# Four convolution tiles on TensorE quadrants, a triangular corner product, the convolution's layer norm inside the chunk loop, and its output layer right behind the loop

## The chip, the cores and the metric

The kernel runs on one core of a Trainium2 chip. Its engines work beside each other: TensorE (PE in the profile, PEld its weight loads), VectorE (DVE), ScalarE (ACT), GpSimd (POOL), and SyncE (SP), whose queue issues most DMAs. They meet only at semaphores. The metric is the device time of one execution in microseconds; a lower time is better. Differences below about 0.2% can't be told from no change.

## What is computed

Two blocks of a language model over 256 tokens with 1024 features in float32. The change lies in the first block, which mixes a recurrent head layer (RWKV) with a convolution branch:

```python
def conformer_conv(p_c, dw, dw_b, ln_w, ln_b, w_o):
    u, gate = jnp.split(p_c, 2, axis=-1)
    c = u * jax.nn.sigmoid(gate)
    c = <causal depthwise convolution of c with dw, 31 taps> + dw_b
    c = jax.nn.silu(layer_norm(c, ln_w, ln_b))
    return c @ w_o

# end of rwkv7_time_mix: y (per head) from the recurrence wkv7
    y = ((y - mu) * lax.rsqrt(var + GN_EPS)) * gn_w + gn_b      # mean and variance per head
    return ((y + bonus) * g) @ w_o                             # bonus = (sum of r*k*r_k) * v

    merged = sigmoid(z_rwkv) * y_rwkv + sigmoid(z_conv) * y_conv
    x = x + rms_norm(merged @ w_out, post_mix_norm)
```

The recurrence runs over 8 chunks of 32 tokens. Inside a chunk it needs the inverse of a unit lower-triangular 32x32 matrix for each of 16 heads and 8 chunks.

## The kernel before

Activations lie transposed: a tile is 128 features by 256 tokens, and 1024 features are 8 tiles, one `slot` of the array `pj`. A large product (`pe_layer`) goes in blocks of 128 output columns. The weights of a block are split into a high part by ACT (`act_head`, L476) and a rest by DVE (`dve_rest`, L482), and PE makes 24 products of 128x256 for the block (L441 to L443; L2215 to L2217 for the layer `z`, which is spread over the chunk loop). Sums in plain float32 (`mm`) cost two records each in the trace.

The order is written out by hand, engine by engine; semaphores tie the programs together. Around the change it is this.

- Ahead of the loop DVE makes the gated input of the convolution (L1533) and signals it. PE then convolves three tiles of it (`PE_TILES = 3`): for each tap one float32 product with a 128x128 diagonal matrix as weights (L2268), 31 to a tile. ACT makes the diagonals from the identity matrix (`tap_weights`, L920) in a ring of 12 and brings the sums out (`conv_tile`, L924).
- Meanwhile DVE ends the inverses. The two 16x16 diagonal blocks are done by substitution (L1492, L1494), the corner by two triple products in 4 slabs each (`slab`, L1478 a product of 128x1024 and L1479 its sum). Both factors are triangular, and the slabs use their full squares.
- PE turns the inverses (L2279), then the chunk loop begins. DVE convolves the other five tiles: of its 31 taps, 11 ahead of the loop (`DVE_EARLY`), and the rest behind the chunk work of the first six iterations, `DVE_TAPS = (4, 4, 3, 3, 3, 3)`. A tap is one instruction a tile (L1550). `scale_keys(1)` (L1568) stands ahead of the last three early taps; PE's `chunk_keys(1)` waits for it.
- One iteration on PE: x from the last state (L2293, L2297), `chunk_keys` (L2126), two blocks of `z`, y from the old state (L2308), u (L2320), `chunk_products` of the next chunk (L2239), the state's update (L2331), y from this chunk (L2335). DVE copies half of u (L1600), masks the products (L1559) and adds to the state (`state_sum`, L1575), which the next x waits for.
- The layer norm of the convolution: its mean is summed on PE in iteration 6 (L2121) and subtracted on DVE in iteration 7 (L1597); ACT squares it there.
- Behind the loop, in this order on PE: the sum for the variance (L2121), the mean per head (`head_sums`, L2115), the bonus (L2346), the variance per head of squares made by POOL (L707), and only then the layer `conv_out`. Beside these DVE scales, centres and multiplies, ACT makes a sigmoid and a linear form of each tile (L973, L974), then the roots of the head norm (L986). The rest of the head norm (POOL L709, ACT L995, DVE L1652 and L1654) lies beside `conv_out`, and `rwkv_out` takes its result.

## Time and profile before

| | us |
|---|---|
| median of 3 runs | 1449.87 (1447.17 to 1450.07) |
| the profiled execution, device time | 1448.39 |
| its span in the trace | 1446.7 |
| PE busy | 1363.5 (94%) |
| DVE busy | 1036.3 (72%) |
| ACT busy | 766.1 (53%) |
| POOL busy | 110.3 (8%) |

The span runs from the first to the last instruction in the trace; 1.7 us of the device time lie around it. The times of all rows are microseconds from the start of the span. A matmul's own time in the trace holds some 0.2 us of latency and overlaps the next, so PE's pace is read from starts.

### The profile page before, as it was taken

The page shows a single profiled execution, that of the slowest core. Times are in us where ns is not written, and L with a number is a line of the kernel's source. Part 1 is how long each engine was busy: PE and PEld are TensorE (multiplying, and loading weights), DVE is VectorE, ACT ScalarE, POOL GpSimd, SP SyncE. Part 2 cuts the span into 40 slices and gives each one's busy share as a digit, 9 for nine tenths or more (in the row PEclk, how much of TensorE's full clock was granted, in tenths as well). Part 3 has the DMA queues.
Part 4 walks back from the last instruction along what each step waited for, and adds up shares of the span by engine and source line. Part 5 has one row for each costly group of instructions (what it writes and reads, how often), then busy time and mean ns, then how long its engine had stood idle before and what let it go on. Part 6 is the DMA issues. An engine that isn't in the chain of part 4 may idle for free.

```text
span 1446.7 us, 29631 instructions
## 1 busy us (share of the span) xinstructions
PE 1363.5 (94%) x12191; PEld 1303.9 (90%) x12191; DVE 1036.3 (72%) x1707; ACT 766.1 (53%) x1262; POOL 110.3 (8%) x127
## 2 busy tenths in 40 slices
PE   6998999898799999999998899999999989999998
PEld 6997988897698999998998699999999978999986
DVE  5769798995677666458598977787565655787754
ACT  5584384334655544345467655544454545644543
POOL 2000000000200211000010100211000100011100
PEclk9999999998899999999999899999999999999999
DMA  8634510120154563854484245554765621455462
GB/s 263 185 97 137 174 61 2 61 90 31 59 175 146 177 192 98 263 182 149 140 249 131 88 147 175 175 174 128 227 193 154 208 84 59 148 191 185 161 212 79
DMA packets 199151, 211.55 MB, mean 146 GB/s; under 512 B 8634, under 2 KB 190666, under 8 KB 198874
## 3 DMA queue, kind: packets, MB, share of 16 engines
q1 hardware_dynamic: 196938, 201.39, 43.8%
q0 software_dynamic: 2000, 8.46, 2.0%
q8 instruction: 88, 1.44, 0.4%
q14 instruction: 29, 0.24, 0.0%
q10 hardware_dynamic: 96, 0.02, 0.0%
HBM read 208.22 MB, written 1.64 MB: 145 GB/s over the span
## 4 chain that ended last, share of the span: by engine, by line
PE 76%; DVE 12%; issue 5%; ACT 3%; DMA 2%; POOL 1%; SPq 0%; DVEq 0%; ACTq 0%; POOLq 0%
PE pb L441 19%; PE pb L443 18%; PE pb L442 18%; PE pb L2268 3%; DVE w_lo L482 2%; DVE pj L1550 1%; PE pb L2586 1%; PE pb L2588 1%; PE pb L2587 1%; PE pb L2126 1%; DMA raw<-in_ffn_w_down_dram 1%; PE pb L2513 1%; PE pb L2169 1%; PE pb L2115 1%; PE pb L2121 1%
## 5 line engine op out<-in xcount | busy, mean ns | idle before, releaser
L441 PE MATMUL pb<-x_hi,w_hi 128*128 128x256 f32 x1984 | 567.1, 286 | 16.7 <-DVE w_lo L482 6.3
L482 DVE TENSOR_TENSOR w_lo<-raw,w_hi 128x1024 fp32r<-128x1024 f32 (+2 forms) x384 | 469.0, 1224 | 157.7 <-ACT w_hi L476 156.9
L476 ACT ACTIVATE w_hi<-raw 128x1024 fp32r<-128x1024 f32 (+2 forms) x384 | 395.7, 1040 | 333.7 <-PE pb L443 251.1
L442 PE MATMUL pb<-x_lo,w_hi 128*128 128x256 f32 x1984 | 563.6, 284 | 0.0
L443 PE MATMUL pb<-x_hi,w_lo 128*128 128x256 f32 x1984 | 563.5, 284 | 0.0
L441 PEld LDWEIGHTS pb<-x_hi,w_hi 128*128 128x128 f32 x1984 | 383.2, 193 | 20.8 <-DVE w_lo L482 11.7
L442 PEld LDWEIGHTS pb<-x_lo,w_hi 128*128 128x128 f32 x1984 | 383.4, 193 | 0.2
L443 PEld LDWEIGHTS pb<-x_hi,w_lo 128*128 128x128 f32 x1984 | 383.1, 193 | 0.0
L716 POOL TENSOR_TENSOR sub<-sub,rstd 128x256 f32<-128x256 f32 x66 | 72.0, 1106 | 575.1 <-ACT sub L1045 575.1
L441 PE MATMUL pb<-act_hi,w_hi 128*128 128x256 f32 x392 | 111.9, 285 | 3.8 <-DVE w_lo L482 3.8
L443 PE MATMUL pb<-act_hi,w_lo 128*128 128x256 f32 x392 | 111.6, 285 | 0.0
L442 PE MATMUL pb<-act_lo,w_hi 128*128 128x256 f32 x352 | 100.3, 285 | 0.0
L1045 ACT ACTIVATE sub<-sub 128x256 f32<-128x256 f32 x66 | 26.5, 415 | 101.1 <-DVE sub L1759 84.4
L441 PEld LDWEIGHTS pb<-act_hi,w_hi 128*128 128x128 f32 x392 | 76.0, 194 | 4.3 <-DVE w_lo L482 4.3
L443 PEld LDWEIGHTS pb<-act_hi,w_lo 128*128 128x128 f32 x392 | 75.9, 194 | 0.0
L442 PEld LDWEIGHTS pb<-act_lo,w_hi 128*128 128x128 f32 x352 | 68.3, 194 | 0.0
L1730 DVE TENSOR_TENSOR sub<-pb,rstd 128x256 f32<-128x256 f32 x66 | 27.8, 423 | 45.8 <-PE pb L443 43.4
L1550 DVE SCALAR_TENSOR_TENSOR pj<-pj,par 128x255 f32<-128x255 f32 (+29 forms) x150 | 59.6, 464 | 0.8
L1736 DVE TENSOR_TENSOR sub<-pb,sub 128x256 f32<-128x256 f32 x66 | 27.7, 420 | 39.7 <-PE pb L443 22.2
L1336 DVE TENSOR_TENSOR pj<-pb,rstd 128x256 f32<-128x256 f32 x72 | 30.3, 422 | 31.5 <-PE pb L443 30.1
L1052 ACT ACTIVATE act_hi<-sub 128x256 f32 (+1 forms) x66 | 27.3, 416 | 45.1 <-DVE sub L1736 44.8
L2126 PE MATMUL pb<-ident,pj 128*128 128x128 f32 (+1 forms) x218 | 37.1, 313 | 8.2 <-DMA pj<-in_x_dram 6.0
(340 smaller groups left out, 2186.1 us busy)
## 6 DMA issues: line engine op xcount, KB each, us to landing
raw<-in_ffn_w_up_dram SPq DMA_DIRECT2D x55, 1024.0 KB, 5.1
raw<-in_w_in_dram SPq DMA_DIRECT2D x28, 1024.0 KB, 5.1
raw<-in_ssd_w_in_dram SPq DMA_DIRECT2D x20, 1024.0 KB, 5.4
raw<-in_ffn_w_down_dram SPq DMA_DIRECT2D x16, 1024.0 KB, 5.3
raw<-in_fox_w_in_dram SPq DMA_DIRECT2D x16, 1024.0 KB, 5.7
raw<-in_ffn_w_down_dram SPq DMA_DIRECT2D x16, 896.0 KB, 5.3
raw<-in_ffn_w_gate_dram SPq DMA_DIRECT2D x11, 1024.0 KB, 5.3
raw<-in_ssd_w_out_dram SPq DMA_DIRECT2D x8, 1024.0 KB, 5.5
```

Source lines behind the costliest of these rows:

```text
L441: pe.matmul(o, w_hi[m][:, k, :], hi[:, k0 + k, :], start=first and k == 0, stop=False)
L442: pe.matmul(o, w_hi[m][:, k, :], lo[:, k0 + k, :], start=False, stop=False)
L443: mm = pe.matmul(o, w_lo[m][:, k, :], hi[:, k0 + k, :], start=False, stop=final and k == nk - 1)
L476: act.activation(piece(ly, w_hi[m], nk, m), raw_piece(ly, s, nk, m), ACT.Copy).then_inc(sem("w_hi_ready"), 1)
L482: dve.tensor_tensor(piece(ly, w_lo[m], nk, m), raw_piece(ly, s, nk, m), piece(ly, w_hi[m], nk, m).bitcast(F32), ALU.subtract).then_inc(sem ...
L716: pool.tensor_tensor(s_tile[m], s_tile[m], rstd[:, :], ALU.mult).then_inc(sem("glu_silu"), 1)
L1336: tt(o, pb[m][:, 0:T], rstd[:, :], ALU.mult).then_inc(sem("evac_done"), 1)
L1550: go(stt(o[:, s:T], c[:, 0:T - s], w, o[:, s:T], ALU.mult, ALU.add))
L1730: tt(g_tile[m], pb[m][:, 0:T], rstd[:, :], ALU.mult).then_inc(sem("evac_done"), 1)
L1736: tt(a_tile[m - 2], pb[m][:, 0:T], s_tile[m - 2], ALU.mult).then_inc(sem("evac_done"), 1)
L2126: return pe.transpose(o, i, ident[0:n, 0:n])
L2268: mm(pb[4 + k % 2][:, s:T], diag[(CONV_TAPS * k + s) % NDIAG], slot(U)[:, k, 0:T - s], start=s == 0, stop=s == CONV_TAPS - 1, skip_group_c ...
```

## The change

Six parts.

1. `PE_PAIRS = 2`: PE convolves four tiles, in two pairs. For `ug`, the layer that makes u and gate, the weight pieces of units 0 and 2 are taken in another order of columns (`raw_piece`), so that of a pair's 256 features the tile c holds those with a = 0, 1 at partitions 64a, of which the convolution's outputs are partitions 64c of bank a. A tap of a pair is four products of 64x64 weights, one to each quadrant of the array. The weights are 64 columns wide (`ident2`, `conv_dw_pe`), two tiles of them to a tap, in a ring of 24.
2. DVE convolves four tiles, 15 taps ahead of the loop, 16 in iterations 0 to 3.
3. The corner: the slabs leave out what the triangles make zero; shapes go from 4x16x16 down to a quarter. The evacuations of the first two `z` blocks move ahead of it.
4. The layer norm: mean in iteration 4, variance and root in iteration 5, scaling in iteration 6, all sums in bank 5, and a Silu of ACT instead of sigmoid, linear form and product.
5. Behind the loop PE makes the bonus and the head mean, then begins `conv_out`; the head variance is summed behind its second block. The squares go from POOL to ACT, the root's product from POOL to DVE. The rows of `z_rwkv` get their sigmoid in iteration 4.
6. Five DMAs more on SP in the load of the parameters (four of `conv_dw_pe`, one for a split row), ahead of the third weight unit.

PE, where the convolution begins. Before, from the products of chunk 0 on:

```order
L2239 MATMUL pb<-pj 64x64 x16
L2126 MATMUL pb<-ident,pj 128x128 x8
L2268 MATMUL pb<-pj 128x256
L2268 MATMUL pb<-pj 128x255
L2268 MATMUL pb<-pj 128x254
```

Now:

```order
L2292 MATMUL pb<-pj 64x64 x16
L2179 MATMUL pb<-ident,pj 128x128 x8
L2324 MATMUL pb<-pj 64x256 x4
L2324 MATMUL pb<-pj 64x255 x4
L2324 MATMUL pb<-pj 64x254 x4
```

A tap is four products of 64 columns for two tiles, where it was one product of 128 for one; 62 such groups stand where 93 products stood.

DVE, the early taps and `scale_keys(1)` ahead of the loop. Before:

```order
L1550 SCALAR_TENSOR_TENSOR pj<-pj,par 128x249 x5
L1568 TENSOR_TENSOR pj<-pj,chunk_decay 128x512
L1550 SCALAR_TENSOR_TENSOR pj<-pj,par 128x248 x5
L1550 SCALAR_TENSOR_TENSOR pj<-pj,par 128x247 x5
L1550 SCALAR_TENSOR_TENSOR pj<-pj,par 128x246 x5
L1526 TENSOR_TENSOR pj<-pb,rstd 128x256 x2
```

Now:

```order
L1599 SCALAR_TENSOR_TENSOR pj<-pj,par 128x245 x4
L1617 TENSOR_TENSOR pj<-pj,chunk_decay 128x512
L1599 SCALAR_TENSOR_TENSOR pj<-pj,par 128x244 x4
L1599 SCALAR_TENSOR_TENSOR pj<-pj,par 128x243 x4
L1599 SCALAR_TENSOR_TENSOR pj<-pj,par 128x242 x4
L1575 TENSOR_TENSOR pj<-pb,rstd 128x256 x2
```

The scaling of the keys of chunk 1 stood behind 8 taps of 5 instructions, and stands behind 12 taps of 4.

PE, the end of the loop and what follows. Before:

```order
L2320 MATMUL pb<-pj 32x64 x16
L2335 MATMUL pb<-pj 64x32 x16
L2121 MATMUL pb<-pj,ones 128x256 x8
L2115 MATMUL pb<-pj,blk 128x256 x8
L2346 MATMUL pb<-small,ident 64x256 x16
L2115 MATMUL pb<-sub,blk 128x256 x8
L441 MATMUL pb<-x_hi,w_hi 128x256
```

Now:

```order
L2375 MATMUL pb<-pj 32x64 x16
L2396 MATMUL pb<-pj 64x32 x16
L2402 MATMUL pb<-small,ident 64x256 x16
L2168 MATMUL pb<-pj,blk 128x256 x8
L445 MATMUL pb<-x_hi,w_hi 128x256
```

Two of the four sums between the loop and `conv_out` are gone from there: one is in the loop, one behind two blocks of the layer.

```diff
-        PE_TILES, NDIAG, DIAG_LEAD = 3, 12, 8
-        diag = [slot(ZC)[:, i // 2, P * (i % 2):P * (i % 2) + P] for i in range(NDIAG)]
+        PE_TILES, NDIAG, DIAG_LEAD = 2 * PE_PAIRS, 24, 8
+        diag = [slot(ZC)[:, i // 4, HEAD * (i % 4):HEAD * (i % 4) + HEAD] for i in range(NDIAG)]
-        DVE_TAPS = (4, 4, 3, 3, 3, 3)
+        DVE_TAPS = (4, 4, 4, 4)
+        LN_SUM, LN_VAR, LN_SCALE = len(DVE_TAPS), len(DVE_TAPS) + 1, len(DVE_TAPS) + 2
...
+            if ly.name == "ug" and u % PE_PAIRS == 0:
+                pair = raw[s][:, 0:nk, 2 * P * (m // 2):2 * P * (m // 2) + 2 * P]
+                return pair.rearrange("p k (a c i) -> p k a c i", c=2, i=HEAD)[:, :, :, m % 2, :]
... POOL
-            pool.tensor_tensor(tmp2, slot(R), slot(R), ALU.mult).then_inc(sem("pool_stages"), 1)
-            pool.tensor_tensor(slot(R), slot(R), slot(TMP), ALU.mult).then_inc(sem("pool_stages"), 1)
... ACT: the diagonals
-                    act.activation(diag[n % NDIAG], ident[:, :], ACT.Copy, scale=par_col("conv_dw", KC * (CONV_TAPS - 1 - s) + k)).then_inc(sem("tap_ready"), 1)
+                    for c in range(2):
+                        n = 2 * (CONV_TAPS * q + s) + c
+                        if n >= NDIAG and c == 0:
+                            act.wait_ge(sem("tap_summed"), (n - NDIAG) // 2 + 1)
+                        act.activation(diag[n % NDIAG], ident2[:, :], ACT.Copy,
+                                       scale=par_col("conv_dw_pe", 2 * (CONV_TAPS * q + CONV_TAPS - 1 - s) + c)).then_inc(sem("tap_ready"), 1)
... ACT: inside the loop
+                if c == LN_SUM:
+                    act.wait_ge(sem("evac_done"), L["z"].evac0 + BANKS + KC)
+                    act.activation(slot(ZR), slot(ZR), ACT.Sigmoid).then_inc(sem("z_ready"), 1)
+                if c == LN_VAR:
+                    log_exp()
+                    act.wait_ge(sem("ln_centred"), 2)
+                    act.activation(slot(U), slot(GATE), ACT.Square).then_inc(sem("ln_act"), 1)
+                if c == LN_SCALE:
+                    for m in range(2):
+                        act_head(act, L["conv_out"], 0, 0, m)
+                    for k in range(KC):
+                        if k % 4 == 0:
+                            act.wait_ge(sem("ln_ready"), k // 4 + 1)
+                        act.activation(slot(GATE)[:, k, :], slot(GATE)[:, k, :], ACT.Silu, scale=par_col("conv_ln_w", k),
+                                       bias=par_col("conv_ln_b", k)).then_inc(sem("ln_act"), 1)
                 act.wait_ge(sem("u_done"), c + 1)
... ACT: beside conv_out
+            def gn_stages(u, m):
+                if (u, m) == (0, 0):
+                    <4 squares of 128x512, as the head mean is subtracted>
+                if (u, m) == (0, 1):
+                    <8 products of g with gn_w>
+                if (u, m) == (0, 2):
+                    <wait for the variance; 4 pairs of Ln and Exp of 128x512>
+                if (u, m) in ((0, 3), (1, 0)):
+                    <4 tiles each of y_hi>
... DVE: the corner
-                rows = left[:, r, :].unsqueeze(2).broadcast_to([P, SLAB, BLOCK, BLOCK])
+            def corner_columns(i):
+                n, r = SLAB * (i + 1), slice(SLAB * i, SLAB * i + SLAB)
+                products(lt_corner[:, :, r], lt_corner[:, :, 0:n], mt[:, BLOCK:BLOCK + n, BLOCK + SLAB * i:BLOCK + n], (BLOCK, SLAB, n))
+            def corner_rows(i):
+                r, j = slice(SLAB * i, SLAB * i + SLAB), slice(SLAB * i, BLOCK)
+                products(mt_corner[:, r, :], mt[:, r, j], lt_corner[:, j, :], (SLAB, BLOCK, BLOCK - SLAB * i))
... DVE: inside the loop
+                if c == LN_SCALE:
+                    dve.wait_ge(sem("ln_act"), 2)
+                    for h in range(2):
+                        tt(cv[:, 4 * h:4 * h + 4, :], cv[:, 4 * h:4 * h + 4, :], rs[:, :].unsqueeze(1).broadcast_to([P, 4, T]),
+                           ALU.mult).then_inc(sem("ln_ready"), 1)
...
+                if c == LN_SUM:
+                    dve.wait_ge(sem("ln_mean"), 1)
+                    ts(rs[:, :], pb[5][:, 0:T], 1.0 / D, None, ALU.mult).then_inc(sem("ln_centred"), 1)
+                    dve.wait_ge(sem("ln_centred"), 1)
+                    tt(cv, cv, rs[:, :].unsqueeze(1).broadcast_to([P, KC, T]), ALU.subtract).then_inc(sem("ln_centred"), 1)
... PE
-                    mm(pb[4 + k % 2][:, s:T], diag[(CONV_TAPS * k + s) % NDIAG], slot(U)[:, k, 0:T - s],
+                    for c in range(2):
+                        for a in range(2):
+                            ins = mm(pb[4 + 2 * q + a][side[c], s:T], diag[(2 * i + c) % NDIAG][side[a], :],
+                                     slot(U)[side[a], 2 * q + c, 0:T - s], start=s == 0, stop=s == CONV_TAPS - 1, skip_group_check=True)
...
+                if c == LN_SUM + 1:
+                    pe.wait_ge(sem("ln_centred"), 1)
+                if c == LN_VAR + 1:
+                    pe.wait_ge(sem("ln_act"), 2)
...
+                if c == LN_SUM:
+                    pe.wait_ge(sem("conv_ready"), PE_TILES + 1)
+                    feature_sums(pb[5][:, 0:T], slot(GATE)).then_inc(sem("ln_mean"), 1)
+                if c == LN_VAR:
+                    pe.wait_ge(sem("ln_act"), 1)
+                    feature_sums(pb[5][:, 0:T], slot(U)).then_inc(sem("ln_var"), 1)
...
+            def group_sums(u, m):
+                if (u, m) == (0, 1):
+                    pe.wait_ge(sem("gn_act"), 4)
+                    head_sums(tmp2, 4).then_inc(sem("gn_var"), 1)
```

In angle brackets stands in words what the lines do.

## Rows read from the trace of the kernel before

**Rows 1.** The page: busy tenths of 40 slices, with PE's granted clock.

```profile
PE   6998999898799999999998899999999989999998
PEclk9999999998899999999999899999999999999999
```

**Rows 2.** Stretches: start:end, length, busy of PE, PEld, DVE, ACT, POOL; clock, DMA.

```profile
188.90:237.30 48.40, 47.06 (x455) 43.39 (x459) 47.18 (x65) 34.93 (x91) 0.53 (x1) 0.96 0.08 25
...
296.20:308.80 12.60, 12.49 (x283) 11.91 (x286) 12.04 (x25) 5.95 (x12) 0.00 (x0) 1.00 0.19 58
...
340.10:349.40 9.30, 4.86 (x161) 4.36 (x161) 7.22 (x7) 6.14 (x10) 0.00 (x0) 0.67 0.20 57
349.40:377.60 28.20, 18.99 (x80) 14.29 (x80) 16.59 (x32) 22.26 (x37) 3.71 (x1) 0.74 0.06 20
```

**Rows 3.** PE in order of time: start, length, line, tiles, shape, count [idle before].

```profile
188.92 39.77 PE L2268 MATMUL pb<-pj 128*128 128x256 f32 x186 [3.21 <-DVEq L1534]
...
237.22 0.69 PE L2293 MATMUL pb<-pj 32*32 32x64 f32 x32 [0.74 <-issue]
238.22 1.06 PE L2126 MATMUL pb<-ident,pj 128*64 128x128 f32 x8
...
282.26 1.91 PE L2126 MATMUL pb<-ident,pj 128*64 128x128 f32 x8
```

**Rows 4.** PE in order of time, products on parts of the array.

```profile
340.88 0.46 PE L2297 MATMUL pb<-sub,pj 64*32 64x64 f32 x32
...
358.45 3.67 PE L2346 MATMUL pb<-small,ident 16*64 16x256 f32 x32
```

**Rows 5.** ACT in order of time.

```profile
11.54 3.29 ACT L776 ACTIVATE x_hi<-x_res,par 128x256 fp32r<-128x256 f32 x8
...
182.71 3.60 ACT L920 ACTIVATE pj<-ident,par 128x128 f32<-128x128 f32 x12
```

**Rows 6.** DVE in order of time: the corner, early taps, state sums.

```profile
184.87 0.95 DVE L1492 TENSOR_TENSOR sub<-sub 128x450 f32<-128x450 f32 x1
185.86 0.62 DVE L1494 TENSOR_REDUCE sub<-sub 128x30 f32<-128x450 f32 x1
...
192.26 1.98 DVE L1478 TENSOR_TENSOR sub<-sub 128x1024 f32<-128x1024 f32 x1
194.27 1.22 DVE L1479 TENSOR_REDUCE sub<-sub 128x64 f32<-128x1024 f32 x1
195.52 1.99 DVE L1478 TENSOR_TENSOR sub<-sub 128x1024 f32<-128x1024 f32 x1
...
236.59 0.69 DVE L1568 TENSOR_TENSOR pj<-pj,chunk_decay 128x512 f32<-128x512 f32 x1
237.20 6.13 DVE L1550 SCALAR_TENSOR_TENSOR pj<-pj,par 128x248 f32<-128x248 f32 x15
...
249.90 0.69 DVE L1575 TENSOR_TENSOR sub<-sub,pb 128x512 f32<-128x512 f32 x1 [0.21 <-DVE pj L1559]
...
295.32 0.69 DVE L1575 TENSOR_TENSOR sub<-sub,pb 128x512 f32<-128x512 f32 x1 [0.22 <-PE pb L2331]
```

**Rows 7.** PE in order of time, behind the loop.

```profile
347.44 1.92 PE L2335 MATMUL pb<-pj 64*64 64x32 f32 x32 [4.33 <-issue]
349.29 5.78 PE L2121 MATMUL pb<-pj,ones 128*128 128x256 f32 x16
354.91 3.62 PE L2115 MATMUL pb<-pj,blk 128*128 128x256 f32 x16
...
377.60 0.58 PE L441 MATMUL pb<-x_hi,w_hi 128*128 128x256 f32 x1 [5.98 <-ACT pj L986]
```

**Rows 8.** PE in order of time, the last block of `conv_out` and `rwkv_out`.

```profile
401.70 0.58 PE L441 MATMUL pb<-x_hi,w_hi 128*128 128x256 f32 x1 [2.30 <-DVE w_lo L482]
...
405.63 0.28 PE L441 MATMUL pb<-x_hi,w_hi 128*128 128x256 f32 x1
405.98 0.28 PE L441 MATMUL pb<-y_hi,w_hi 128*128 128x256 f32 x1
```

More of the change, by code:

```diff
@@ L678, in _ @@
             sync()
+            for h in range(2):
+                rows = slice(HEAD * h, HEAD * h + HEAD)
+                link(pool.tensor_copy(ident2[rows, :], ident[rows, rows]))
             for b in range(4):
@@ L941, in _, with conv_heads @@
                                pb[4 + i][:, :].rearrange("p (t y) -> p y t", y=32), ACT.Copy).then_inc(sem("inverse_rows"), 1)
+            def conv_heads(first, last):
+                act.wait_ge(sem("block_done"), L["z"].item1 + BANKS)
+                for k in range(first, last):
+                    act.wait_ge(sem("ln_act"), 2 + k + 1)
+                    act.activation(x_hi[:, k, :], slot(GATE)[:, k, :], ACT.Copy).then_inc(sem("x_hi_ready"), 1)
             v_rows(0)
@@ L992, in y_heads @@
+            log_exp()
+            def gn_stages(u, m):
+                if (u, m) == (0, 0):
+                    for b in range(4):
+                        act.wait_ge(sem("gn_dve"), 4 + b + 1)
+                        act.activation(tmp2[:, 2 * b:2 * b + 2, :].rearrange("p k t -> p (k t)"), pair(R, b), ACT.Square).then_inc(sem("gn_act"), 1)
                 if (u, m) == (0, 1):
-                    act.wait_ge(sem("pool_stages"), GN_ROOTED)
                     for k in range(KC):
-                        act.activation(slot(R)[:, k, :], slot(R)[:, k, :], ACT.Identity, scale=par_col("gn_w", k),
-                                       bias=par_col("gn_b", k)).then_inc(sem("gn_root"), 1)
@@ L997, in y_heads @@
-                if (u, m) == (0, 3):
-                    act.wait_ge(sem("mix_in"), KC + 1)
-                    for k in range(KC):
-                        act.activation(y_hi[:, k, :], slot(R)[:, k, :], ACT.Copy).then_inc(sem("x_hi_ready"), 1)
-            act_layer(act, L["conv_out"], y_heads, nxt=L["rwkv_out"])
+                        act.activation(slot(U)[:, k, :], slot(G)[:, k, :], ACT.Copy, scale=par_col("gn_w", k)).then_inc(sem("gn_act"), 1)
+                if (u, m) == (0, 2):
+                    act.wait_ge(sem("gn_var"), 1)
+                    for b in range(4):
+                        link(act.activation(pair(TMP, b), pb[4 + b][:, :], ACT.Ln, bias=eps[:, 2:3], scale=1.0 / HEAD))
+                        act.activation(pair(TMP, b), pair(TMP, b), ACT.Exp, scale=-0.5).then_inc(sem("gn_root"), 1)
@@ L1003, in mixed_head @@
+                if (u, m) in ((0, 3), (1, 0)):
+                    for b in range(2 * u, 2 * u + 2):
+                        act.wait_ge(sem("mix_in"), b + 1)
+                        for k in (2 * b, 2 * b + 1):
+                            act.activation(y_hi[:, k, :], slot(R)[:, k, :], ACT.Copy).then_inc(sem("x_hi_ready"), 1)
+            act_layer(act, L["conv_out"], gn_stages, nxt=L["rwkv_out"])
             def mixed_head(j):
-                act.wait_ge(sem("mix_in"), KC + 1 + j + 1)
+                act.wait_ge(sem("mix_in"), 4 + j + 1)
```

219 lines of the change are left out of this document (103 added, 116 removed).

## The prediction

> **What bounds the kernel now.** I read the page's slices first: PE is busy nearly everywhere, with its clock granted in full (2.4 GHz, digit 9), but for the tenth and eleventh slice, 326 to 398 us, where the clock digit is 8 and PE's own are 8 and 7 (once more near 800 us, in another part) [rows 1]. So the kernel is PE-bound outside, and only what shortens PE's own path there, or fills its gaps, counts. The table by stretches shows where the path is thin [rows 2]. From 188.9 to 237.3 PE and DVE are both full: PE convolves (39.77 us for 93 taps) [rows 3] and then turns the inverses, DVE works 47.2 of 48.4 us. In the loop a good iteration takes 12.6 us, PE and DVE both over 12. The last one and the stretch behind the loop (28.2 us) are not full on any engine: a chain of small steps handed from engine to engine, with a mean clock of 0.67 and 0.74, so for half of the time or more at the lower level, 1.2 GHz. Everything from `rwkv_out` on (406.0 us) [rows 8] is untouched by the diff, so the gain is the lead with which that layer starts. I follow this lead past six marks.
>
> **1. The corner on DVE.** A slab costs 3.26 us from product to next product (192.26 to 195.52) [rows 6]; there are eight, 26.1 us. Now their sizes are 1024, 768, 512, 256, twice. The pair of 450 elements (0.95 and 0.62) and the pair of 1024 (1.98 and 1.22) [rows 6] give lines through which I read 2.55, 1.8 and 1.1 us for the smaller ones, gaps included. Sum 2 x 8.75 = 17.5 us, so DVE is 8.6 us earlier. Ahead of `scale_keys(1)` stand 48 tap instructions now, not 40, at 6.13 / 15 = 0.41 us each [rows 6]: 3.3 us back. It ended at 237.3 and ends at 232.1, a lead of 5.2. The moved evacuations (two instructions) cost DVE the same either way.
>
> **2. The taps on PE.** The taps take 0.40 to 0.43 us each for a full-width product of some 240 columns (39.77 / 93) [rows 3]. A tap of a pair is four products of 64x64, and the question is how many run at once. The nearest row is L2297: 16 products of 64 columns on tiles of 64x32, eight places of the array, 0.46 us from the first start to the last end [rows 4]. One full-width product of 64 columns would be 0.107 us at the taps' pace, sixteen 1.7 us. So rows and columns of the array both work in parallel, far more than fourfold. L2346, 256 columns long but on two places only, takes 3.67 / 16 = 0.23 us a product, half of 0.43 [rows 4], so long products share too. I take full concurrency: 62 taps at 0.405, plus the 2.3 us that the low clock costs at the start (39.77 less 93 x 0.403), 27.4 us. PE is through at 216.5, not 228.7. Bounds: two at a time, 0.81 us (the L2346 case), and one at a time, 1.62. The Trainium skill, page "TensorE: Matmul & The Clock Gate", section "Measured speedup vs the span model", has 3.07 times for four tiles in four row groups, not 4. By that a tap would be 0.53 us, the taps 7.5 us longer, and the sum the same within 1 us, because of the slack in the next paragraph; no row here has four places.
>
> **ACT must feed it.** A scaled copy costs 0.41 us at 256 columns and 0.30 at 128 (3.29 / 8, 3.60 / 12) [rows 5]; I extrapolate 0.24 to 0.25 for 64. Per tap of a pair 0.48, slower than PE's 0.405, but 12 taps lie ready when PE starts (24 of them, 5.7 us, fit between 182.7 and 188.9), and with two weight pieces first, ACT falls behind only at the very end: about 216.5 too. If the narrow copy gained nothing (0.30), ACT ends at 221.5.
>
> **3. Where the loop starts.** From the end of the taps to x of chunk 0 it was 8.5 us (228.7 to 237.2) [rows 3], so x now begins at 225.1, keys(1) a microsecond later, and there PE **waits for DVE's `scale_keys(1)` until 232.1**: the 12 us that the quadrants win are cut to a lead of 6.1 (keys(1) started at 238.2) [rows 3]. This is the slack that hides a slower tap, up to 0.5 us a tap. The idle 6 us cost clock: after such a gap the same eight turns took 1.91 us, not 1.06 [rows 3], and the first products behind them ran slow too; 1.7 us. `state_sum(0)` came 11.7 us behind the start of the keys (249.9) [rows 3, 6], now at 245.5: lead 4.4.
>
> **4. Iterations 0 to 3** are set by DVE. Between state sums 0 and 3 lay 45.4 us (249.90 to 295.32) [rows 6] with 20, 20 and 15 tap instructions; now 16 each, 7 fewer, 2.9 us: 42.5. I take 14.0 us each, 42.0, since in the third PE, not DVE, came last ("<-PE L2331") and had a gap to close. Lead 7.8.
>
> **5. Iterations 4 to 7.** They took 54.0 us (295.3 to 349.4) [rows 6, 7] with one sum of 8 tiles in it, 3.6 us at full clock, as the like sum L2115 took [rows 7], and the 4.3 us idle of PE ahead of its last products [rows 7]. Now a second sum comes in (+3.6); PE waits for the mean to leave bank 5, behind `state_sum(4)` (+1.1), and for ACT in iteration 6, which makes eight Silus ahead of its copies of u (+0.8). The first two waits hold back x and all behind it on PE; ACT's Square, table load and root fit beside two blocks of `z`. Gone are the 4.3 us idle and about 2.5 us of low clock (clock 0.67 in the last iteration) [rows 2]. DVE has no taps there any more. Sum -1.3: 52.7 us, lead 9.1, loop end 340.3.
>
> **6. Behind the loop** 28.2 us [rows 2, 7] become the bonus, 3.67 [rows 4], and the head mean, 3.62 [rows 7]: 7.3 us. The tiles of x_hi and x_lo (8 x 0.3 on ACT, 8 x 0.34 on DVE) fit beside. Low clock may come back, as L2121 took 5.78 at the same place where the like sum took 3.62 [rows 7]; I put 1 us. Gain 28.2 - 8.3 = 19.9, lead 29.0, `conv_out` starts near 348.5. It took 28.4 us (377.60 to 405.98) with a wait of 2.30 for weights and a slow start [rows 7, 8]; now 8 blocks at 24 x 0.12 = 2.88 us (405.63 to 405.98 is three products) [rows 8] and the variance sum, 3.6: 26.7. Lead **30.7**.
>
> What else is there costs nothing as I see it. In `conv_out` DVE has some 8 x 0.34, 12 x 0.6 and 8 x 0.34 us of head norm between eight weight rests and eight gates, about 27 in 26.7 + the next layer's slack; the nearest deadline, the rests of block (1,2), is met by 2 us. SP issues five small DMAs more at about 0.35 us, 1.8 us, with PE's turn of the parameters near behind; between 0 and 2 us, I take 0, since the weights that follow are wanted much later. The other order of columns in `raw_piece` changes no size.
>
> **The sum.** 1446.7 - 30.7 = 1416.0 of span, with 1.7 around it 1417.7 against the profiled 1448.39. The median is 1.5 above that run, so the forecast is **1419**.
>
> **Rivals.** (a) *Two quadrants at a time*: 0.81 us a tap. For it speaks that no row has four places at this length; against it L2297. PE is through at 241.4, keys(1) begin 9.5 later without a gap, `state_sum(0)` at 262.6: 17 later than forecast, 1436. (b) *Quadrants one after another*, since each product adds to a bank that another one writes: 1.62 us a tap, 62 taps 100 us, `state_sum(0)` near 312, **slower, 1486**. It decides from 1.03 us a tap on, where 62 taps end at 255.0 and `state_sum(0)` comes at 276.2, 30.7 behind forecast. L2297 writes banks the same way and speaks against it. (c) *ACT feeds too slowly*: at 0.40 us a copy, as a paced one might take, 50 pairs are 40 us, PE is through at 232, +8: 1427. (d) *The head norm beside `conv_out` is late*, DVE's queue holding a weight rest behind a wait for ACT's roots: 2 to 6 us, 1423. (e) *The loop is better than I think*: PE follows DVE without the low clock, -4 us: 1415. (f) That the change doesn't shorten the chain at all: no, two of the four sums and POOL's two steps are gone from it.
>
> **Chances.** Forecast with (d) and (e), which are its margins: 0.80; (c) 0.06; (a) 0.09; (b) 0.03; something unseen of 5 to 25 us 0.02. The range takes the forecast's margins and (c), and the lower half of (a): 1411 to 1434. Faster by over 0.2% (about what a measurement of this kernel can tell) 0.95, same 0.01, slower 0.04.
>
> **What would show it.** Taps: 62 groups from 188.9 that end near 216.5; if they end near 241, (a). An idle of PE of about 6 us ahead of keys(1), ended by DVE's scaling; without it step 3 is wrong. Corner 17.5 us. State sums near 245.5 and 287.5. Bonus right behind the loop, `conv_out` near 348.5 and `rwkv_out` near 375, without a POOL row between. I would be wrong most of all by PE's clock, which I only take from like places, and by the waits in iterations 4 to 6.

## The result

The changed kernel takes **1424.66 us** (median, 1423.21 to 1429.6), the kernel before 1448.62 us in the same series: ratio 0.9857, 95% interval 0.9831 to 0.9883. It is faster, as forecast, and 5.7 us above the 1419 that were named, inside the range. The profiled run has a span of 1424.0 us, and 8.0 us more than the 1416.0 of the sum have to be found in it.

The page's slices of the changed kernel, the ones of [rows 1] again:

```profile
PE   5999997999999999999998899999999998999998
PEclk8999998998999999999999899999999999999999
```

The weak place of two slices is now one, the tenth (320 to 356 us, clock digit 8). But the first slice went from 6 to 5 with clock digit 8, and the seventh (214 to 249 us), which was at 9 with full clock, is at 7 with clock digit 8: that is PE's wait ahead of the loop. In order of time (start, length in us, engine, line, tiles, count, idle before and who ended it), first SP's queue and PE at the start of the kernel, then PE from the taps to the loop, then one state sum of DVE and the second product of u in iteration 7, with all that stands between it and `conv_out`:

```profile
13.40 6.67 SPq L597 DMA_DIRECT2D pj<-in_conv_dw_dram  x6
25.28 0.52 SPq L597 DMA_DIRECT2D pj<-in_ffn_conv_b_dram  x1
27.11 1.51 PE L2179 MATMUL pb<-ident,pj 128*128 128x128 f32 x6 [3.51 <-DMA pj<-in_ffn_conv_b_dram]
...
192.71 27.26 PE L2324 MATMUL pb<-pj 64*64 64x256 f32 x496 [2.12 <-DVEq L1583]
219.90 6.03 PE L2335 MATMUL pb<-ident,sub 128*32 128x32 f32 x256
236.05 1.92 PE L2179 MATMUL pb<-ident,pj 128*64 128x128 f32 x8 [7.16 <-DVE pj L1617]
250.45 0.69 DVE L1624 TENSOR_TENSOR sub<-sub,pb 128x512 f32<-128x512 f32 x1 [0.21 <-DVE pj L1608]
...
347.06 1.24 PE L2396 MATMUL pb<-pj 64*64 64x32 f32 x32 [0.96 <-DVE pj L1650]
348.23 7.09 PE L2402 MATMUL pb<-small,ident 16*64 16x256 f32 x32
355.25 5.14 PE L2168 MATMUL pb<-pj,blk 128*128 128x256 f32 x16
360.03 0.47 PE L445 MATMUL pb<-x_hi,w_hi 128*128 128x256 f32 x1
```

Read against [rows 3, 6 to 8], the leads over the kernel before are, in us:

| mark | forecast | changed kernel | run e11 (below) |
|---|---|---|---|
| weight blocks on PE and DVE behind the start (36 us) | 0 | -5.0 | -2.0 |
| the taps on PE begin | 0 | -3.8 | -2.0 |
| `state_sum(0)` | 4.4 | -0.5 | 4.0 |
| `state_sum(3)` | 7.8 | 2.5 | 7.7 |
| end of the loop | 9.1 | 1.1 | 10.6 |
| `conv_out` starts | 29.0 | 17.6 | 28.6 |
| `rwkv_out` starts | 30.7 | 19.3 | 30.3 |
| end of the span | 30.7 | 22.7 | 29.2 |

So four things came late: the start (3.8 us where the taps begin), the clock between the keys of chunk 1 and `state_sum(0)` (1.0 more than forecast), the iterations 4 to 7 (2.8), and the stretch behind the loop (3.4). The rest of the table is as forecast. The start itself was 5.0 us late; some 1.2 of it was gone before the taps, most of it at one place. The data of the inverses go out to DRAM and back, and DVE waits for them. The same two transfers took 11.9 us before and 10.9 now; what made them shorter stays open. First a weight rest of DVE behind the start and the second transfer before, then the same now:

```profile
31.34 1.23 DVE L482 TENSOR_TENSOR w_lo<-raw,w_hi 128x1024 fp32r<-128x1024 f32 x1
...
154.79 7.38 DMA sub<-sub_in
```

```profile
36.38 1.23 DVE L491 TENSOR_TENSOR w_lo<-raw,w_hi 128x1024 fp32r<-128x1024 f32 x1 [0.67 <-ACT w_hi L485]
...
159.53 6.49 DMA sub<-sub_in
```

Behind `rwkv_out`, where both kernels run the same instructions, the lead grew by 3.4 us. That part isn't the change's: over the profiled runs of this study the same part gave between -1.1 and +6.1 us, with the clock of a few stretches (0.93 from 720 to 800 us here, 0.91 in the same work before). It is also why medians of kernels that differ by 2 or 3 us overlap. Below, the marks in the traces decide, and the times are given beside them. The marks scatter too: in seven profiled runs whose instructions are the same up to the taps, these begin between 192.7 and 193.5 us, and in two others with one start (e11, e12) 1.5 us apart. Of the times alone, only e7's interval lies clear of the changed kernel's.

### The profile page after: what moved, and what is told of

The parts are those of the page before. It is cut to its first block, busy times and chain, and to the rows that moved or that the text cites. A ratio compares the mean times of both kernels' runs of the same rounds, so it can differ in the third digit from the quotient of the medians.

```text
span 1424.0 us, 30260 instructions
## 1 busy us (share of the span) xinstructions
PE 1348.2 (95%) x12502; PEld 1280.9 (90%) x12502; DVE 1013.9 (71%) x1680; ACT 762.1 (54%) x1294; POOL 102.4 (7%) x127
## 4 chain that ended last, share of the span: by engine, by line
PE 78%; DVE 13%; issue 4%; ACT 2%; DMA 2%; SPq 2%; DVEq 0%; ACTq 0%; POOLq 0%
PE pb L445 20%; PE pb L447 19%; PE pb L446 19%; DVE pj L1599 2%; DVE w_lo L491 2%; PE pb L2646 1%; PE pb L2645 1%; PE pb L2644 1%; PE pb L2179 1%; PE pb L2168 1%; SPq L597 1%; DMA raw<-in_ffn_w_down_dram 1%; PE pb L2571 1%; PE pb L2268 1%; PE pb L2269 1%
## 5 line engine op out<-in xcount | busy, mean ns | idle before, releaser
L485 ACT ACTIVATE w_hi<-raw 128x1024 fp32r<-128x1024 f32 (+2 forms) x384 | 396.2, 1040 | 336.9 <-PE pb L447 256.8
L1783 DVE TENSOR_TENSOR sub<-pb,rstd 128x256 f32<-128x256 f32 x66 | 27.7, 423 | 46.6 <-PE pb L447 43.9
L1789 DVE TENSOR_TENSOR sub<-pb,sub 128x256 f32<-128x256 f32 x66 | 27.7, 419 | 39.8 <-PE pb L447 22.2
L1091 ACT ACTIVATE act_hi<-sub 128x256 f32 (+1 forms) x66 | 27.3, 416 | 44.7 <-DVE sub L1789 44.7
L2179 PEld LDWEIGHTS pb<-ident,pj 128*128 128x128 f32 (+1 forms) x219 | 28.3, 153 | 24.2 <-issue 8.9
```

The costliest lines, as they stand in the source:

```text
L485: act.activation(piece(ly, u, w_hi[m], nk, m), raw_piece(ly, u, s, nk, m), ACT.Copy).then_inc(sem("w_hi_ready"), 1)
L1091: act.activation(o, a_tile[m], ACT.Copy).then_inc(sem("act_hi_ready"), 1)
L1783: tt(g_tile[m], pb[m][:, 0:T], rstd[:, :], ALU.mult).then_inc(sem("evac_done"), 1)
L1789: tt(a_tile[m - 2], pb[m][:, 0:T], s_tile[m - 2], ALU.mult).then_inc(sem("evac_done"), 1)
L2179: return pe.transpose(o, i, ident[0:n, 0:n])
```

## The experiments

Each is the changed kernel with one edit, unless it says otherwise. The state sums (us from the span's start) of all the runs, the end of the loop, and the start of `conv_out`:

| | sum 0 | 1 | 2 | 3 | 4 | 5 | 6 | loop ends | `conv_out` | median us | ratio to before, interval |
|---|---|---|---|---|---|---|---|---|---|---|---|
| changed | 250.5 | 264.4 | 279.0 | 292.8 | 308.6 | 328.6 | 342.1 | 348.3 | 360.0 | 1424.66 | 0.9857, 0.9831 to 0.9883 |
| e1 | 249.6 | 263.6 | 277.5 | 291.3 | 307.0 | 324.1 | 337.6 | 345.9 | 359.2 | 1423.49 | 0.9855, 0.981 to 0.9899 |
| e2 | 248.3 | 265.1 | 279.6 | 293.4 | 309.1 | 326.2 | 339.7 | 347.6 | 359.7 | 1426.01 | 0.9859, 0.9819 to 0.9898 |
| e3 | 250.0 | 264.4 | 278.3 | 293.9 | 310.0 | 326.2 | 339.7 | 346.0 | 357.9 | 1420.84 | 0.9826, 0.9787 to 0.9865 |
| e4 | 250.6 | 265.2 | 279.1 | 293.3 | 309.4 | 326.5 | 340.0 | 354.3 | 360.5 | 1425.91 | 0.9854, 0.9812 to 0.9896 |
| e5 | 248.0 | 262.4 | 276.3 | 291.9 | 308.1 | 326.7 | 340.2 | 348.3 | 360.1 | 1425.36 | 0.9849, 0.9815 to 0.9883 |
| e6 | 248.6 | 263.1 | 277.0 | 292.6 | 308.7 | 327.3 | 340.8 | 348.9 | 360.7 | 1426.91 | 0.9858, 0.9823 to 0.9893 |
| e7 | 258.3 | 272.7 | 286.6 | 302.2 | 318.3 | 336.9 | 350.4 | 358.6 | 370.3 | 1435.4 | 0.993, 0.9904 to 0.9956 |
| e8 | 248.4 | 262.3 | 276.2 | 290.0 | 305.8 | 322.9 | 336.4 | 342.1 | 354.0 | 1421.28 | 0.9842, 0.9807 to 0.9877 |
| e9 | 248.5 | 262.4 | 276.3 | 290.1 | 305.9 | 324.5 | 338.0 | 343.7 | 355.5 | 1423.14 | 0.9832, 0.9813 to 0.9852 |
| e10 | 245.5 | 259.4 | 273.3 | 287.1 | 302.9 | 321.5 | 335.0 | 344.0 | 355.9 | 1422.82 | 0.9831, 0.98 to 0.9862 |
| e11 | 245.9 | 259.9 | 273.7 | 287.6 | 303.3 | 319.4 | 333.0 | 338.8 | 349.0 | 1419.5 | 0.9811, 0.9788 to 0.9835 |
| e12 | 244.5 | 259.1 | 273.4 | 287.3 | 303.0 | 319.1 | 332.7 | 341.9 | 353.9 | 1420.57 | 0.9812, 0.9789 to 0.9835 |

### The start: e1, e5, e6

e1 issues the four loads of `conv_dw_pe` on ACT's queue, e5 leaves them on SP's but last of the list, e6 puts them on POOL's:

```diff
 e1, e6: load_params(sp, range(1, par_tiles), "par_loaded", pairs=False)
 e1: @block.scalar, behind par_first
+    load_params(act, range(1, par_tiles), "par_loaded", pairs=True)
 e5: behind the list without them
+    load_params(sp, range(1, par_tiles), "par_loaded", pairs=True)
 e6: @block.gpsimd, behind the constants
+    load_params(pool, range(1, par_tiles), "pairs_loaded", pairs=True)
```

> The four loads of the pair-ordered convolution weights (62 rows of two-way split 256-byte pieces, 15.5 KB each) are issued on ACT's queue at the start of the kernel and no longer on SP's queue ahead of weight unit 2; nothing else changes. Theory A (SP's issue of these four is what makes the start 5.0 us later): SP's last parameter load is issued near 19 to 20 us instead of 25.3, PE's turn of the parameters comes without its idle of 3.5 us, everything behind is 4 to 5 us earlier, the time 1420 us (4.5 less than the changed kernel's 1424.7). Rival B (the extra cost is the transfers' own, small pieces that hold up whatever shares the DMA engines): the loads then delay x or the first weight unit instead, and the time stays at 1424 to 1427.

> The four loads of the pair-ordered convolution weights stay on SP's queue but come last of the parameter loads, behind ffn_conv_b, at about 19 us. Theory A (an issue of such a load is long only while the DMA engines are full with weights, to 19 us here; on SP in the changed kernel four took about 5.8 us, on ACT's queue in the run before 9.7 us): there, with the DMA engines nearly idle, each takes 0.4 to 0.5 us, the last parameter lands at 23 to 24 us instead of 27.1, and all behind is 3 us earlier: 1421.5. Rival B (the issue is long for its 62 pieces of 256 bytes themselves, 1.4 us or more each wherever it stands): the last parameter lands at 26 to 27 us and the time is the same, 1424.

> The four loads of the pair-ordered convolution weights are issued on POOL's queue, behind its constants (7.7 us), where POOL waits for squares until 17.7 us; SP's list is then that of the kernel before, but one more piece each of conv_b, conv_w. Theory A (the 5.0 us at the start come from the issue of these four alone): the last parameter lands near 21 to 22 us, PE's turn of the parameters is not waited for, everything behind is 4 to 5 us earlier, 1420. Rival B (POOL's own issue takes as long as on the other queues, 9 us and more, and its sum of squares comes later): 1424 or later.

e1 in order of time, the four loads on ACT's queue:

```profile
3.23 9.72 ACTq L599 DMA_DIRECT2D pj<-in_conv_dw_dram  x4
```

e5, the same on SP's queue, and PE's turn of the parameters:

```profile
19.40 2.72 SPq L599 DMA_DIRECT2D pj<-in_conv_dw_dram  x4
...
24.92 1.51 PE L2182 MATMUL pb<-ident,pj 128*128 128x128 f32 x6 [1.37 <-DMA pj<-in_conv_dw_dram]
```

e6, the loads on POOL's queue, and the turn:

```profile
8.51 5.29 POOL L599 DMA_DIRECT2D pj<-in_conv_dw_dram  x4 [0.87 <-POOL g_mask L703]
...
25.53 1.48 PE L2182 MATMUL pb<-ident,pj 128*128 128x128 f32 x6 [2.03 <-DMA pj<-in_ffn_conv_b_dram]
```

The kernel before, its last parameter load and its turn:

```profile
19.11 0.32 SPq L582 DMA_DIRECT2D pj<-in_ffn_conv_b_dram  x1
...
23.75 0.70 PE L2126 MATMUL pb<-ident,pj 128*128 128x128 f32 x5
```

The prediction priced an issue at 0.35 us. Four loads of 62 pieces of 256 bytes took 5.9 us on SP in the changed kernel (6.67 less 0.78 for the two plain ones), 9.7 on ACT at the very start, and 2.7 at 19.4 us, when the DMA engines moved 27 GB/s. So the same issue costs 0.7 us with nearly idle DMA engines, 1.5 on average on SP and 2.4 on ACT while weights are being fetched (307 to 389 GB/s in those stretches of e1). Short pieces aren't the only cause of a long issue: the plain load of `gn_b`, right behind four weight loads, took 2.95 us in both kernels. The Trainium skill ("Perfetto Trace Analysis", section "DMA Instruction — HWDGE (DVE, Sync)") has the profiled time of a DMA instruction include the wait for the descriptor generator and the making of all its descriptors, and the DMA engines' own work not. No row here separates these parts; what the rows show is that the issue of one and the same load depends on what the DMA engines are doing.

e1 undid nothing: ACT held its own first work back for as long (DVE's first rest of the weights, right behind ACT's first high part, came 4.1 us later), and the first weight rest behind the turn stands at 29.49 us, where it was at 29.46. But e5 and e6, in which SP's list ended at 22.1 and 20.4 us instead of 25.8, were only 1.7 and 1.1 us earlier at the last rest ahead of the taps, not 3 or 5. Theory A was right on the issue and wrong on the whole. The turn of the parameters still takes 1.5 us, as in the changed kernel, not the 0.70 of the kernel before: PE has been idle, the granted clock is 0.50, there are six tiles to turn and not five, and the weight products behind it start 0.21 us apart, not 0.12. e10 (below) separates the two: filled with products nobody reads, PE turned the parameters in 0.87 us at 26.9, and the work was 1.7 us earlier right behind and 2.2 at the taps, with the landing only 0.2 earlier. e11, filled and loaded as e5, was 3.1 us earlier right behind, but only 1.8 at the taps, since there the transfers of the inverses' data took 12.5 us, and 10.9 in the changed kernel; e12, with the same start, was 3.3 earlier. **So some 2 of the 5.0 us are clock; the rest is the landing, of which reordering the loads brought 1 to 2 at the marks.** None of it shows in the times: e5 and e6 lie 0.7 and 2.3 us above the changed kernel by the medians.

### PE's wait ahead of the loop: e2, e7, e8, e9

e2 scales the keys behind 7 early taps; e7 computes the corner in full; e8 takes 18 taps of PE twice (the convolution it computes is then another one); e9 puts 14 products nobody reads in PE's wait.

```diff
 e2
-conv_taps(0, DVE_EARLY - 3); scale_keys(1); conv_taps(DVE_EARLY - 3, DVE_EARLY)
+conv_taps(0, DVE_EARLY - 8); scale_keys(1); conv_taps(DVE_EARLY - 8, DVE_EARLY)
 e7
 <both corner products with shape (SLAB, BLOCK, BLOCK), for all slabs>
 e8
-for c in range(2):
+for c in (0, 1, 0, 1) if q == 0 and 2 <= s < 20 else (0, 1):
 e9, in iteration 0 ahead of chunk_keys(1)
+for _ in range(14):
+    mm(pb[6][:, 0:T], ones[:, :], slot(U)[:, 0, :], start=True, stop=True)
```

> The corner's eight slabs are computed in full again (1024 products each, their halves of zeros included, as in the kernel before), all else as in the changed kernel. Theory A (DVE alone sets when the loop gets under way, through scale_keys(1) and the taps behind it): scale_keys(1) ends at 244.7 instead of 236.1, PE's idle ahead of keys(1) grows to 15.8 us, state_sum(0) comes 8.6 us later, 259.2, and the time is 1433. Rival B (other waits of the loop give part of it back): less than 5 us later, 1429 or below.

e7 confirms who sets the start of the loop. PE's wait for the scaling in e7, in order of time (13.89 us, it was 7.16):

```profile
244.68 1.92 PE L2179 MATMUL pb<-ident,pj 128*64 128x128 f32 x8 [13.89 <-DVE pj L1617]
```

The scaling comes 8.6 us later, `state_sum(0)` 7.8 and `conv_out` 10.3, and the median is 10.7 higher. What DVE does ahead of the loop counts in full.

> DVE scales the keys of chunk 1 behind 7 early taps instead of 12; the number of taps ahead of the loop stays 15. Theory A (PE's idle of 7.2 us ahead of keys(1) delays z, y1 and u of iteration 0, and DVE then waits for them): PE's wait shrinks to under 1 us, z of iteration 0 begins near 229 instead of 237.7, DVE comes out of its taps at 241 as now and finds z and u ready; state_sum(0) at 246.5 to 247.5 instead of 250.6, and the time is 3 to 4 us less, 1421. Rival B (DVE sets the start of the loop whatever the order, because the 15 taps are there in either case): state_sum(0) moves by under 1 us and the time stays within 1 us of 1424.7.

e2: the wait went where theory A said, `state_sum(0)` came only 2.2 us earlier, and iteration 1 took 16.9 us instead of 13.9. Nothing is left at `state_sum(1)`. PE of e2 in order of time:

```profile
241.69 1.92 PE L2369 MATMUL pb<-pj,sub 64*64 64x32 f32 x32 [5.85 <-DVE pj L1575]
```

Two stretches of e2 (start:end, length, busy of PE, PEld, DVE, ACT, POOL, granted clock, DMA):

```profile
240.00:245.00 5.00, 3.31 (x72) 3.08 (x74) 2.20 (x7) 0.27 (x1) 0.00 (x0) 0.50 0.00 0
...
250.00:255.00 5.00, 5.00 (x81) 4.40 (x77) 4.89 (x13) 1.82 (x5) 0.00 (x0) 0.50 0.02 3
```

The wait wasn't gone but moved: PE has its `z` done by 235.8 and now waits 5.85 us for DVE's taps to end. The clock is at the lower level (0.50, so 1.2 GHz) to about 255 us, and the work behind it pays. Neither theory had that. The time didn't fall (1426.01).

> 18 of the 62 taps on PE (those of number 2 to 19 of the first pair of tiles) are multiplied and added twice, so the convolution's result of tiles 0 and 1 is not the reference's; PE has 7.3 us more work in the convolution. Theory A (PE's lead there is spent waiting for DVE's scale_keys(1) in any case): PE ends its taps at 227.3 instead of 220.0, its idle of 7.2 us ahead of keys(1) is gone, state_sum(0) comes where it came (250.6) or up to 2 us earlier since the clock no longer falls in the idle time, the time is 1422.5 to 1424.7. Rival B (PE's end of the taps does matter): 7 us later, 1432.

> Ahead of keys(1) PE issues 14 products of 256 columns whose result nobody reads (lower half of bank 6, 0.43 us each, 6.0 us in all), where it now sits idle for 7.2 us. Theory A (the run with 18 taps taken twice was faster because the idle of PE there costs clock: keys 1.91 us instead of 1.06, z of iteration 0 in 7.7 us instead of 5.75): the time falls as it did there, state_sum(0) comes near 248.4 instead of 250.6, the time is 1421, and the granted clock of 235 to 245 us is 1.0. Rival B (there it was the later end of the taps, or a better draw of the low-clock stretches in the loop, that helped): state_sum(0) comes as before, the time stays at 1424.

e8, in which PE does **more** (34.58 us of taps, not 27.26), is the test of both. Its keys, in order of time:

```profile
236.66 1.06 PE L2179 MATMUL pb<-ident,pj 128*64 128x128 f32 x8
```

Those of e9:

```profile
236.76 1.06 PE L2184 MATMUL pb<-ident,pj 128*64 128x128 f32 x8 [0.42 <-DVE pj L1617]
```

And a stretch of e8, whose granted clock was 0.50 in the changed kernel:

```profile
235.00:240.00 5.00, 4.41 (x93) 4.18 (x94) 4.90 (x13) 2.81 (x7) 0.00 (x0) 1.00 0.01 3
```

7.3 us of added work cost nothing, and `state_sum(0)` came 2.1 us earlier (2.0 in e9, with the whole result right). The slack of step 3 is real. What the idle time in it costs is read from the start of these keys to `state_sum(0)`: 11.7 us in e8, e9, e10, e11 and e12, where PE doesn't idle ahead of them, as in the kernel before; 13.0 to 14.1 in e1 and e3 to e7, with the idle time, and 14.4 in the changed kernel. So it costs 1.3 to 2.7 us of clock, and the changed kernel's draw was the worst. At the marks a gain stays a gain: e8 and e9 have 13.8 to 14.0 us in each of iterations 1 to 3. In the times it isn't shown: 1421.28 and 1423.14, with intervals that overlap the changed kernel's; e9 was forecast at 1421.

### The layer norm's mean: e3

```diff
     mask_products(c + 1)
+    if c == LN_SUM: <wait for ln_mean, rs = pb[5] / D>
     state_sum(c)
```

> In iteration 4 DVE reads the layer norm's mean out of bank 5 ahead of state_sum(4) (where it sits idle for 2.1 us) instead of behind scale_keys(6). Theory A (PE's idle of 0.9 us ahead of x(5) is what drops the clock, so that x, keys and z of iteration 5 take 1.10, 1.91 and 7.4 us instead of 0.69, 1.06 and 5.75): x(5) starts 0.9 us earlier and at full clock, state_sum(5) comes 17 us behind state_sum(4) instead of 20.1, the time is 3 us less, 1421.5. Rival B (the clock falls in iteration 5 for what PE did before, the many small products, not for this idle): only the 0.9 us is gained, 1423.8.

The changed kernel in order of time, what PE waits for ahead of x of iteration 5:

```profile
310.33 1.10 PE L2354 MATMUL pb<-pj 32*32 32x64 f32 x32 [0.91 <-DVE rs L1664]
```

A stretch of the changed kernel behind it, with its clock:

```profile
314.00:319.00 5.00, 5.00 (x32) 5.00 (x32) 0.71 (x2) 4.19 (x4) 0.00 (x0) 0.68 0.00 0
```

The same product in e3:

```profile
310.84 0.69 PE L2355 MATMUL pb<-pj 32*32 32x64 f32 x32
```

Read from all the runs, the step from state sum 4 to 5 takes 16.1 us in the three runs with this edit (e3, e11, e12), 17.1 us in four without it (e1, e2, e4, e8), and 18.6 or 20.1 in the six others. So the wait costs 1.0 us by itself, which is what step 5 had for it, and in six of ten profiled runs the clock falls behind it as well, for 1.5 to 3.0 us more. Theory A has it, but as a risk, not a rule. The clock falls in other places as well: the step from state sum 2 to 3 takes 15.6 us in e3, e5, e6 and e7 and 13.8 in eight runs, with a granted clock of 0.50 for some microseconds (280 to 284 us in e3). e3 lost 1.8 us there.

### The clock behind the loop: e4, e10, e11, e12

```diff
 e4, in iteration 7
+    <4 bonus products ahead of u, 12 behind u>
 e10: as e9, and
+    <7 products of 128 columns ahead of the first sum of squares, 7 behind it>
+    <2 products of 256 columns ahead of the wait for the rows of u, iterations 6 and 7>
 e11: as e10, with the edits of e5 and e3
 e12: as e11, and the bonus
-    <16 products with 64 columns of the array (ident[0:16, h:h + 1] broadcast to 64)>
+    <8 products with 128, their pattern written by POOL in iteration 6>
```

> The 16 bonus products are issued within iteration 7, 4 of them ahead of the products of u and 12 behind, instead of behind the loop. Theory A (the lower clock behind the loop comes from PE's idle moments in iteration 7 while it waits for the copies of x and u, and filling them keeps the clock): the bonus takes about 3.7 us of which 1 lies in gaps, the head mean 3.6 instead of 5.14, conv_out starts 5 us earlier, 1419.5. Rival B (the clock is down in that stretch whatever is issued there, or the products in the loop delay y2 by as much as they save): the bonus takes 7 us, only the 1 us of gaps is gained, 1423 to 1425.

> As e9, and in three more places where PE waits: 7 products of 128 columns ahead of the first sum of squares (PE idle 2.3 us) and 7 behind it, ahead of the turn of the parameters (idle 3.5 us), and 2 of 256 columns ahead of the wait for the rows of u in iterations 6 and 7 (idle 0.9 us each). Theory A (the 5.0 us lost at the start are 3.4 us of later landing and the rest low clock: turn of the parameters 1.51 us instead of 0.70, the weight blocks at 0.21 us a product to about 31 us; the bonus's 7.09 us and the head mean's 5.14 are the low clock of the idle moments in iterations 6 and 7): 1.5 to 2 us less at the start than e9 and 3 to 5 us less behind the loop, 1415 to 1417. Rival B (the filling only keeps the clock for a moment, or comes in the way of the products that wait): 1420 to 1422, as e9.

> As e10, with the four pair-ordered loads last of the parameter loads on SP (as e5) and the layer norm's mean read ahead of state_sum(4) (as e3). Theory A (with PE filled, the clock at the start doesn't fall, and the earlier landing is worth its full 2.5 us; the wait ahead of x(5) costs 0.9 us or, in a run in which the clock falls there, 3): 2.5 to 3.5 us less than e10, 1412 to 1414. Rival B (what is gained early is given back by low-clock stretches of iterations 3 to 5, as in e5, whose lead of 2.8 us at state_sum(0) was 2.3 at state_sum(5) and nothing behind the loop): within 1 us of e10.

> As e11, and the bonus is made by 8 products with all 128 columns of the array (a 16x128 pattern that POOL writes into a free tile in iteration 6) instead of 16 with 64. In e11 PE is busy without a gap from 330 to 350 us, and the clock still falls at about 341, two microseconds into the bonus's products; the bonus takes 5.0 us and the head mean 5.7. Theory A (the clock falls there because of the products' small tiles, 16 rows by 64 columns, with nothing large beside them): with twice the columns per product the fall is later or gone, bonus 3.5 us and head mean 3.6 to 4.5, conv_out starts 2 to 3.5 us earlier than in e11 (348.96), the time is 1416.5 to 1418. Rival B (the small products of iteration 7 ahead of them decide, or the 16 rows do): bonus 5 us or more, head mean 5 to 6, the time within 1 us of e11.

PE in e4, in order of time:

```profile
344.18 1.97 PE L2344 MATMUL pb<-small,ident 16*64 16x256 f32 x8
...
347.10 5.38 PE L2344 MATMUL pb<-small,ident 16*64 16x256 f32 x24
...
352.42 1.92 PE L2408 MATMUL pb<-pj 64*64 64x32 f32 x32
```

PE in e11:

```profile
338.75 5.02 PE L2418 MATMUL pb<-small,ident 16*64 16x256 f32 x32
343.70 5.70 PE L2172 MATMUL pb<-pj,blk 128*128 128x256 f32 x16
```

Three stretches of e11:

```profile
338.00:340.00 2.00, 2.00 (x40) 1.57 (x39) 1.85 (x7) 1.14 (x4) 0.00 (x0) 1.00 1.09 381
340.00:342.00 2.00, 2.00 (x18) 1.20 (x16) 1.54 (x4) 1.98 (x3) 0.00 (x0) 0.73 0.22 62
342.00:344.00 2.00, 2.00 (x11) 0.87 (x8) 0.55 (x2) 1.99 (x2) 0.00 (x0) 0.50 0.00 0
```

PE in e12:

```profile
335.26 1.81 PE L2387 MATMUL pb<-pj,sub 64*64 64x32 f32 x29 [0.52 <-issue]
...
341.88 7.19 PE L2423 MATMUL pb<-small,pj 16*128 16x256 f32 x16
```

In e4 the bonus takes 7.3 us inside the loop, about what it took behind it, and `conv_out` starts where it did: rival B. In e10 the start and the keys keep their clock, and it falls in iteration 7, ahead of the bonus; of the 3 to 5 us that its theory A had behind the loop none came (11.9 us from the loop's end to `conv_out`, 11.7 in the changed kernel). In e11 PE is busy without a gap from 330 us to the end of the bonus, and the clock still falls, at 341 us. So idle moments alone aren't what brings it down there. e12 was to try the 64 columns of the bonus, but can't decide on them: its clock fell at 335 us, at a gap of 0.5 us, ahead of the bonus. It shows only that at the low clock 8 products of 128 columns take as long as 16 of 64 (7.19 us, and 7.09 in the changed kernel). In all the runs the last blocks of `z` are in iteration 6, and small products, sums and at most two products nobody reads follow on PE until `conv_out`. Whether that is the cause wasn't tried; it would need `z` blocks moved behind iteration 6. The fall comes between 335 and 351 us from run to run, and the stretch from the loop's end to `conv_out` takes 10.2 us (e11) to 13.3 us (e1) in the runs with the bonus behind the loop, where 8.3 was forecast; what starts it stays open.

e11 and e12 have the lowest ratios, 0.9811 and 0.9812 of the kernel before (0.9788 to 0.9835 for e11); e11 is some 5 us under the changed kernel by the median, 6.5 by the span, its interval just overlapping. It reaches the marks of the forecast within 1.5 us, `rwkv_out` at 375.7 where 375.3 was forecast, but not its own forecast of 1412 to 1414. Behind `rwkv_out` the three runs with a filled start (e10 to e12) took 1040.8 to 1041.8 us, as the kernel before did (1040.7), and the changed kernel and its nine other runs 1034.6 to 1038.8. Whether the filling does that wasn't tried. It is at least a warning that a lead at a mark isn't yet a gain in time: e10 leads e9 by 3.0 us at `state_sum(0)`, and their medians are 0.3 us apart.

## Why the prediction was right, and where not

**Corner, right.** The first four slabs take 3.29, 2.55, 1.83 and 1.09 us, 8.76 where 8.75 was forecast (the fourth stands behind two weight rests). e7 shows that they are worth what DVE gets. The first slab, the fourth and the scaling of the keys, which ends at 236.0 where 232.1 was forecast, late by the start's 3.8:

```profile
193.43 2.01 DVE L1516 TENSOR_TENSOR sub<-sub 128x1024 f32<-128x1024 f32 x1
...
203.38 0.60 DVE L1516 TENSOR_TENSOR sub<-sub 128x256 f32<-128x256 f32 x1
...
235.30 0.69 DVE L1617 TENSOR_TENSOR pj<-pj,chunk_decay 128x512 f32<-128x512 f32 x1
```

**Taps, right on the quadrants; the total is right by luck.** 27.26 us for 62 taps, forecast 27.4, and the four quadrants run as one: rivals (a) and (b) are out. But the forecast was 25.1 us of products and 2.3 of low clock at the start, and the clock was 1.00 throughout the taps. What took the 2 us was ACT. PE goes at 0.39 to 0.44 us a tap to about 208 us, then at 0.48 to the end, which is ACT's pace (46 copies in 11.09 us). 16 taps in the middle, 13 late ones, and ACT beside these:

```profile
199.67 6.52 PE L2324 MATMUL pb<-pj 64*64 64x240 f32 x128
...
209.80 6.36 PE L2324 MATMUL pb<-pj 64*64 64x246 f32 x104
```

```profile
208.22 11.09 ACT L934 ACTIVATE pj<-ident,par 128x64 f32<-128x64 f32 x46
```

PE's weight loads waited for ACT's copies 23 times, 6.3 us in all. So rival (c) holds in small: the copies cost 0.24 us as forecast, and PE waits for them in the last third of the taps and more, not "only at the very end". In the runs whose clock was low as the taps began (e3 to e6 and e9 to e11) they took 27.5 to 27.7 us, hardly longer, because ACT sets the end; and it cost nothing, because of the wait below. The prediction's reading of L2297 as "far more than fourfold" is too strong for its own figures (1.7 us against 0.46 is 3.7). The Trainium skill's 3.07 ("TensorE: Matmul & The Clock Gate", section "Measured speedup vs the span model") is for four row groups. It does not carry over to this pattern of two row groups by two column groups: before ACT holds PE back, four products take 0.39 to 0.44 us, and one full-width product took 0.40 to 0.43.

**The wait ahead of the loop, right but for 1 us of clock.** 7.16 us, forecast about 6, and the clock loss behind it 2.7 us (1.3 to 2.7 over the runs), forecast 1.7. (The row that priced it, the keys at 282.26 us in [rows 3], stood behind waits of 1.59 and 0.68 us, not behind one of 6.) `state_sum(0)` is 4.9 us late by the start's 3.8 and this 1.0. The sentence that a tap slower by 0.1 us costs nothing was right too (e8). **Iterations 0 to 3, right:** 42.4 us for 42.0. Rival (e), a loop 4 us better, is out for this run.

**The start, wrong: the term of SP's five small loads, "between 0 and 2 us, I take 0", measured 5.0 right behind it and 3.8 at the taps.** The price of 0.35 us a load came from loads of 512-byte rows; those of 256-byte pieces took 0.7 to 2.4 (e1, e5). The prediction named PE's turn of the parameters as near behind, and took 0 because the weights are wanted much later. But the turn waits for the last of these loads: PE goes idle for 3.51 us, and some 2 of the 5.0 us are low clock behind it (e10).

**Iterations 4 to 7, 2.8 us too low.** 52.7 was forecast, 55.5 measured, 54.6 in e1 and 51.2 in e11. The wait for bank 5 cost 1.0, as booked; the fall of the clock behind it, 3.0 in this run and none in e1, was not booked. Of the last iteration's 9.3 us [rows 2] 6.2 are left.

**Behind the loop, 3.4 us too low.** The bonus and the mean stand where they were forecast and no POOL row is between, but at 7.09 and 5.14 us against 3.67 and 3.62, where 1 us was allowed for the clock. The warning was in [rows 7], where the first sum behind the loop took 5.78. The order of the steps was changed, the low clock stayed with the place. Of the 28.2 us from the loop's end to `conv_out` 11.7 are left. No run puts the sums back behind the loop: that this largest part of the gain is theirs is read from the marks, and not shown by an experiment.

**`conv_out`, right.** 26.66 us for 26.7, without a wait; rival (d) is out.

The errors of these terms are nearly all on one side, 11.4 us at `rwkv_out`. The range, 15 us upwards of the forecast, would have held the time in any case; that it came within 5.7 us is due to 3.4 us gained in the layers behind, which no step had.
